# Four transformer layers and a fifth block on one core: the last two output units of the stick-breaking mixers cut in halves around the last group's values

## The reference, cut to what matters

```python
for i in range(4):                                   # then second_block(...)
    mod = silu(c) @ ada_w[i] + ada_b[i]              # 1024 -> 6 * 1024
    sh1, sc1, g1, sh2, sc2, g2 = split(mod, 6)
    h = rms_norm(x, gain[i, 0]) * (1 + sc1) + sh1
    x = x + g1 * mixer(h)                            # i = 0, 3: stick breaking; 1: MoBA; 2: sliding window
    h = rms_norm(x, gain[i, 1]) * (1 + sc2) + sh2
    x = x + g2 * ((silu(h @ w_gate) * (h @ w_up)) @ w_down)

def stick_breaking(h, w_in, w_out):                  # 16 heads of 64
    q, k, v = split(h @ w_in, 3)
    z = q @ k.T / 8
    later = reversed_cumsum(log_keep) - log_keep     # log_keep = log_sigmoid(-z), past keys only
    a = exp(log_sigmoid(z) + later)                  # strictly past keys
    return (a @ v) @ w_out
```

## Time and profile before

| what | value |
|---|---|
| time, median of 3 runs (lowest to highest) | 2160.32 us (2155.64 to 2163.41) |
| the profiled execution: time, span | 2167.3 us, 2165.5 us |
| mean granted TensorE clock | 0.954 |
| TensorE matmul busy | 1952.9 us (90%) |
| VectorE busy | 1344.4 us (62%) |
| ScalarE busy | 918.1 us (42%) |
| GpSimd busy | 111.8 us (5%) |
| matmuls, vector, scalar instructions | 13890, 1412, 1367 |

### The profile page before, as it was taken

One profiled execution on the slowest core, in us unless ns is written; L12 is line 12 of the kernel. 1 busy time (PEld: TensorE's weight loads), 2 busy tenths in 40 slices (PEclk: granted clock), 3 DMA queues, 4 the chain that ended last, 5 costly groups with the idle time before them and its releaser, 6 DMA issues.

```text
span 2165.5 us, 33122 instructions
## 1 busy us (share of the span) xinstructions
PE 1952.9 (90%) x13890; PEld 1522.8 (70%) x13890; DVE 1344.4 (62%) x1412; ACT 918.1 (42%) x1367; POOL 111.8 (5%) x139
## 2 busy tenths in 40 slices
PE   4888999999999998999999899989998888778998
PEld 3665887645687764677777677777786787666877
DVE  6775787453588734688755578875447645445564
ACT  3445444332544324544355544444335211335443
POOL 1001000020100000000000100002000220000000
PEclk9998999999899999999999899998989999989999
DMA  8763898533499931599843267973222000224552
GB/s 325 268 221 95 286 335 323 174 123 116 143 336 315 326 104 59 185 339 314 308 132 121 89 225 254 336 269 128 67 78 78 3 4 4 81 97 149 178 178 97
DMA packets 215114, 393.37 MB, mean 182 GB/s; under 512 B 11306, under 2 KB 130102, under 8 KB 199606
## 3 DMA queue, kind: packets, MB, share of 16 engines
q1 hardware_dynamic: 214453, 391.12, 52.5%
q0 software_dynamic: 512, 0.13, 0.0%
HBM read 390.17 MB, written 1.05 MB: 181 GB/s over the span
## 4 chain that ended last, share of the span: by engine, by line
PE 57%; DVE 25%; ACT 10%; issue 6%; DMA 2%; DVEq 0%; POOL 0%; ACTq 0%; SPq 0%; POOLq 0%
PE G L2126 11%; PE G L2128 11%; DVE w_lo L1426 11%; PE G L2127 11%; DVE acc L1477 6%; PE G L2332 5%; ACT w_hi L931 5%; PE G L2408 2%; PE A L2702 2%; DVE act_st L1760 1%; ACT full L996 1%; DMA raw<-in_ffn_w_down 1%; PE A L2714 1%; PE G L2716 1%; PE A L2174 1%
## 5 line engine op out<-in xcount | busy, mean ns | idle before, releaser
L1426 DVE TENSOR_TENSOR w_lo<-raw,w_hi 128x2048 fp32r<-128x2048 f32 (+2 forms) x237 | 513.4, 2166 | 288.9 <-ACT w_hi L931 277.4
L931 ACT CAST w_hi<-raw 128x2048 fp32r<-128x2048 f32 (+1 forms) x230 | 427.6, 1859 | 553.8 <-PE G L2128 474.7
L2126 PE MATMUL G<-w_hi,h_hi 128*128 128x512 f32 (+2 forms) x1232 | 495.2, 402 | 22.3 <-issue 11.3
L2127 PE MATMUL G<-w_lo,h_hi 128*128 128x512 f32 (+2 forms) x1232 | 485.2, 394 | 0.0
L2128 PE MATMUL G<-w_hi,h_lo 128*128 128x512 f32 (+2 forms) x1232 | 484.8, 394 | 0.0
L1477 DVE SCALAR_TENSOR_TENSOR acc<-raw,c_col,acc 128x2048 f32<-128x2048 f32 x120 | 282.0, 2350 | 20.9 <-DVE w_lo L1426 9.0
L2126 PEld LDWEIGHTS G<-w_hi,h_hi 128*128 128x128 f32 x1232 | 238.5, 194 | 78.4 <-issue 32.7
L2126 PE MATMUL G<-w_hi,act_hi 128*128 128x512 f32 (+2 forms) x640 | 255.4, 399 | 38.1 <-DVE w_lo L1426 28.5
L2128 PEld LDWEIGHTS G<-w_hi,h_lo 128*128 128x128 f32 x1232 | 237.5, 193 | 50.0
L2127 PEld LDWEIGHTS G<-w_lo,h_hi 128*128 128x128 f32 x1232 | 238.2, 193 | 45.9
L2128 PE MATMUL G<-w_hi,act_lo 128*128 128x512 f32 (+2 forms) x640 | 250.2, 391 | 0.0
(11 more groups left out here) (396 smaller groups left out, 2083.9 us busy)
## 6 DMA issues: line engine op xcount, KB each, us to landing
raw<-in_ada_w SPq DMA_DIRECT2D x96, 1024.0 KB, 5.5
raw<-in_ffn_w_gate SPq DMA_DIRECT2D x88, 512.0 KB, 4.0
raw<-in_ffn_w_up SPq DMA_DIRECT2D x88, 512.0 KB, 5.1
raw<-in_ffn_w_down SPq DMA_DIRECT2D x40, 1024.0 KB, 6.5
raw<-in_w_mlp SPq DMA_DIRECT2D x32, 1024.0 KB, 5.4
raw<-in_w_ada SPq DMA_DIRECT2D x24, 1024.0 KB, 5.3
raw<-in_w_in SPq DMA_DIRECT2D x18, 1024.0 KB, 5.3
raw<-in_sb_w_in SPq DMA_DIRECT2D x32, 512.0 KB, 4.6
```

The source lines that it names most:

```text
L931: nc.scalar.copy(w_hi[:, c % 2, 0:len(kts), 0:n], raw[:, slot].rearrange("p (k n) -> p k n", k=UNIT_K)[:, 0:len(kts), 0:n])\
L1426: return nc.vector.tensor_tensor(w_lo[:, c % 2, ks, 0:n], raw[:, slot].rearrange("p (k n) -> p k n", k=UNIT_K)[:, ks, 0:n], w_hi[:, c % 2, ...
L2126: nc.tensor.matmul(banks[t][:, 0:n], x_hi[:, kt, ts], w_hi[:, u % 2, i, 0:n], start=st, stop=False)
L2127: nc.tensor.matmul(banks[t][:, 0:n], x_hi[:, kt, ts], w_lo[:, u % 2, i, 0:n], start=False, stop=False)
```

## The change

- In an sb mixer the first gate's sums (`"r1"`) stand ahead of unit 12 instead of behind unit 13, and ScalarE's copies of them in slot 11 instead of 13. Before T and S of group 3 TensorE waits until they are copied, since these use the same banks.
- Units 14 and 15 are each cut in two halves of 12 matmuls. First the halves with blocks 4 and 5 (group 2) of both units, then V of group 3, then the second gate's sums (`"r2"`), then the halves with blocks 6 and 7 (group 3) of both units. `gemm_done` for each unit comes behind its second half.
- `("V", 3)` moves from slot 13 to slot 14 in `SB_SLOTS`, for TensorE, ScalarE and VectorE alike.
- `ADA_MIX[0]` puts two modulation products in slot 0 and two in slot 5, where it had three in slot 0 and one in slot 5. The products of slots 1 to 4 have indices one lower than before; from slot 6 on they are the same.

```diff
--- before.py
+++ after.py
@@ -417,7 +417,7 @@
 
         SB_SLOTS = {2: [("T", 0)], 3: [("S", 0)], 4: [("C", 0)], 5: [("T", 1)], 6: [("V", 0), ("S", 1)], 7: [("C", 1)],
                     8: [("V", 1), ("T", 2)], 9: [("S", 2)], 10: [("C", 2)], 11: [("V", 2)], 12: [("T", 3), ("S", 3)],
-                    13: [("C", 3), ("V", 3)]}
+                    13: [("C", 3)], 14: [("V", 3)]}
         MOBA_PE = {2: [("N", 0)], 3: [("T", 0)], 4: [("N", 1), ("S", 0)], 5: [("T", 1)], 6: [("N", 2), ("C", 0)], 7: [("S", 1)],
                    8: [("N", 3), ("T", 2), ("C", 1)], 9: [("S", 2)], 10: [("T", 3)], 11: [("V", 0), ("C", 2), ("V", 1)],
                    12: [("V", 2), ("S", 3)], 13: [("C", 3)], 14: [("V", 3)]}
@@ -570,7 +570,7 @@
         ADA_MIX = [{}, {}, {}, {}]
         ADA_FF = [{}, {}, {}, {}]
         for i in range(2 * KT):
-            ADA_MIX[0].setdefault(max(0, i - 2), []).append((0, KT + i))
+            ADA_MIX[0].setdefault((0, 0, 1, 2, 3, 4, 5, 5, 6, 7, 8, 9, 10, 11, 12, 13)[i], []).append((0, KT + i))
         for l in range(DEPTH):
             twice = KT if l + 1 == LAT else 0
             for i in range(ADA_U):
@@ -1146,8 +1146,8 @@
                             squares()
                         for step, g in SB_SLOTS.get(n, []):
                             step_sb(step, g)
-                        if n in (nq + 1, nq + 2):
-                            modulation(l, ("r1", "r2")[n - nq - 1])
+                        if n in (nq - 1, nq + 2):
+                            modulation(l, "r1" if n < nq else "r2")
                     else:
                         for step, g in ACT_STEPS[kind].get(n, []):
                             step_softmax(step, g, kind)
@@ -2356,20 +2356,43 @@
                     unit(h_hi, h_lo, range(4 * h, 4 * h + 4), G[2 * (pns[-1] % 2):2 * (pns[-1] % 2) + 2], h == 0, h == 1,
                          width(panels[pi]), ready=ready_at(f_h, h))
                     steps(n)
+                modulation(l, "r1")
                 po = [k.panel("dve"), k.panel("dve")]
-                n = 2 * len(panels)
-                for h in range(2):
-                    pe.wait_ge(split_lo, f_o[2 * h + 1] - k.native)
-                    for j in range(2):
-                        if h == 0:
-                            wait_panel_free(po[j])
-                        unit(act_hi, act_lo, range(4 * h, 4 * h + 4), G[2 * (po[j] % 2):2 * (po[j] % 2) + 2], h == 0, h == 1, tiles=h == 1 and j == 1)
-                        steps(n)
-                        if n == 2 * len(panels) + 1:
-                            modulation(l, "r1")
-                        if n == 2 * len(panels) + 2:
-                            modulation(l, "r2")
-                        n += 1
+                nq = 2 * len(panels)
+                pe.wait_ge(split_lo, f_o[1] - k.native)
+                for j in range(2):
+                    wait_panel_free(po[j])
+                    unit(act_hi, act_lo, range(4), G[2 * (po[j] % 2):2 * (po[j] % 2) + 2], True, False)
+                    if j == 0:
+                        pe.wait_ge(mod_out, k.sums)
+                    steps(nq + j)
+
+                def half_unit(j, g):
+
+                    u = nth_converted[k.u + j]
+                    pe.wait_ge(hi_ready, u + 1)
+                    pe.wait_ge(lo_ready, u + 1)
+                    for t in range(NT):
+                        bank, ts = G[2 * (po[j] % 2) + t], slice(t * P, t * P + P)
+                        for i in range(2):
+                            kt, part = 2 * g + i, 2 * (g - 2) + i
+                            nc.tensor.matmul(bank, act_hi[:, kt, ts], w_hi[:, u % 2, part], start=False, stop=False)
+                            nc.tensor.matmul(bank, act_hi[:, kt, ts], w_lo[:, u % 2, part], start=False, stop=False)
+                            ins = nc.tensor.matmul(bank, act_lo[:, kt, ts], w_hi[:, u % 2, part], start=False, stop=g == 3 and i == 1)
+                        if g == 3 and j == 1 and t == 0:
+                            ins.then_inc(tile_done, 1)
+                    if g == 3:
+                        ins.then_inc(gemm_done, 1)
+
+                pe.wait_ge(split_lo, f_o[2] - k.native)
+                for j in range(2):
+                    half_unit(j, 2)
+                steps(nq + 2)
+                modulation(l, "r2")
+                pe.wait_ge(split_lo, f_o[3] - k.native)
+                for j in range(2):
+                    half_unit(j, 3)
+                k.u += 2
 
             def softmax_mixer(l, kind):
 
```

## The result

The changed kernel takes 2162.11 us (median of 22 runs, 2156.87 to 2171.55), the kernel before 2159.86 us in the runs beside it (22 runs, 2146.52 to 2165.70). The ratio is 1.0022, 95% interval 1.0012 to 1.0033: slower by about 4.8 us (2.6 to 7.1), within the 0.3% that the prediction called no change, though with 22 runs of each the interval leaves out 0. (The two medians alone differ by 2.3 us, the two means by 4.2; this document goes by the recorded ratio and its interval.) The forecast was +3.6 us, 2163.9.

What follows compares the result with a forecast made beforehand. TensorE was taken to set the pace, so the change is worth what it alters in TensorE's stops. Terms -4.3 + 0 + 4.8 + 3.1 = +3.6 us gave 2163.9 against the median, range 2155 to 2172.

Steps and rivals of the forecast that it cites:

- First slots, -4.3 us: Layer 0, slot 0: two products instead of three start unit 2 2.6 us earlier and avoid a 1.7 us clock loss.
- the first slots give nothing: Rival, chance 0.12: unit 3's load or cast in layer 0 takes back the 4.3 us; total +7.9, 2168.2 us.
- Slot 5, 0: Layer 0: the product moved ahead of kT's copy makes VectorE 0.6 late but costs TensorE 0; without cover, 2.6 us.
- Sums ahead, layer 0: 0, layer 3: +1.7: First gate's sums before unit 12: free in layer 0's 2.23 us idle time, +1.7 us in layer 3, which has no stop.
- Halves, layer 3: +4.8 with the sums: Units 14 and 15 around V of group 3: right half of the norm starts at 1228.5 against 1223.69, +4.8 us.
- wait for `w_lo` 4.2: Layer 3: TensorE idles 4.2 us before unit 15's first half, until its cast and subtraction finish; before, 3.0.
- V's end to the first group 3 half 2.1: Layer 3: the split of V takes 2.1 us before the group 3 halves start, covering the second gate's 1.73.
- that half to the right residual 7.1: Layer 3: rest of unit 14 (2.9), left residual (2.6) and squares (1.6) put the right half 7.1 us later.
- Halves, layer 0: +3.1: Units 14 and 15 around V of group 3: right half of the norm starts at 198.95 against 195.87, +3.1 us.
- `n_st`, 0: Norm behind slot 15: one of two `n_st` is hit by GpSimd's clearing in either kernel; 0, bounds ±1.9 a layer.
- the first `n_st` goes free: Rival, chance 0.13: the first `n_st` escapes GpSimd's clearing, -1.9 us in each layer; total -0.1, 2160.2 us.
- The clock rival, +10.1: Rival, chance 0.17: 1.2 GHz lasts through second half, V and second gate's sums; total +10.1 us, 2170.4.

Runs made afterwards that it cites:

- e1: The kernel before with only the changed ADA_MIX[0] table (two modulation products in slots 0 and 5): 2158.79 us against 2158.59, ratio 0.9998.
- e8: The kernel before with only the changed ADA_MIX[0] table, run again on another chip: 2152.90 us against 2158.52, ratio 0.9976.
- e7: The kernel before with only the first gate's sums moved ahead of unit 12: one execution of 2159.06 us.
- e2: The changed kernel with the old ADA_MIX[0] table, so the second edit alone: 2167.55 us against 2158.59 for before, ratio 1.0039.
- e5: The changed kernel with GpSimd's last two clearings held until the norm's scaled rows are done: 2160.92 us against 2158.52 for before, ratio 1.0010.
- e4: The kernel before with the new ADA_MIX[0] and, on TensorE alone, only unit 14 halved around V of group 3: 2148.17 us against 2158.59, ratio 0.9945.
- e9: Before with new ADA_MIX[0], unit 14 alone halved, GpSimd's clearing late, and VectorE's slot 12 kT copy ahead of the modulation product: one execution, 2142.26 us.

## Why the prediction came out right

**First slots, -4.3 us: right.** TensorE's stop fell to 1.13 us and the stretch behind it ran at 1.00 where 0.76 stood; unit 2 started at 54.69, forecast 54.4. The whole is 4.4 us by the date of V of group 2, and 3.5 by the timings of e1 and e8. The rival "the first slots give nothing" is out.

**Slot 5, 0: right.** The two products stand at 88.53 and 91.10; the copy of kT, reckoned to start 2.6 late, and the split of V follow, and at V of group 2 the first edit's gain is whole on the mean of the kernels.

**Sums ahead, layer 0: 0, layer 3: +1.7: right as the change makes it.** In layer 0 unit 12 starts 3.78 us behind V of group 2, before it was 3.80. The 1.7 of layer 3 is e7's 1.68. My expectation for e7 alone was wrong by 3 us, for the second stop.

**Halves, layer 3: +4.8 with the sums, measured +5.25** (57.62 - 52.37; in e2 +6.0). The steps: wait for `w_lo` 4.2 forecast, 3.81 measured; clock 1.7, measured 1.7; V's end to the first group 3 half 2.1, measured 2.1; that half to the right residual 7.1, measured 1220.64 - 1213.32 = 7.3. No step is off by more than 0.4. (Behind V the working has a slip that changes nothing: from 1209.7 to 1211.73 are 2.0 us, not 2.1.)

**Halves, layer 0: +3.1, whose steps hold and whose base doesn't.** Wait 6.6 forecast, 6.38 measured; clock 2.8, measured 5.35 x 0.50 + 3.86 x 0.09 = 3.0; the residual 195.16 - 187.88 = 7.3 us behind the half. The table has +2.0 (63.4 - 61.4), and after had luck in S of group 3, which took 1.88 us to unit 13 where it took 3.44 before: +3.5 without that. (Of the nine profiles with the same stop ahead of S, after's is the only one in which S kept the full clock.) But before's own profile was a long one behind V: against e1 and e8 it lost 2.8 us to the clock instead of 1.5 and 1.6, and its second `n_st` took 2.62 instead of 1.15 and 0.88. Against these two, with S alike, the halves cost +6.1 and +6.3. I had taken one execution's 2.8 and 2.62 as the kernel's. By e1 and e8 as the base the whole change sums to -4.4 + 5.25 + 6 = +7, by before's own profile to -4.4 + 5.25 + 3.5 = +4.4; timed is +4.8 (2.6 to 7.1). So the mechanism held step by step, but that the total came out within 1.2 us of the timed one is in part luck: layer 0's base scatters by 4 us from execution to execution (61.4, 58.7, 57.1), the forecast had only the highest of them to go by, and the interval is wide enough for either sum.

**`n_st`, 0: right for the profiled execution of before, and its rival "the first `n_st` goes free" is out.** The first one took 2.62 us in layer 0 and 2.76 in layer 3, so it did not go free. Against e1 and e8 it is up to 1.7 us in layer 0, inside the bound of 1.9 given.

**The clock rival, +10.1: not seen in after.** The low level ended in the half (layer 3) or just behind it (layer 0); V and the sums ran at 1.00 and 0.91. It is near, though: in e2 and e5 the whole half of layer 3 ran at 0.50, and V came 0.9 us later there. Two of three kernels with this order lost that, so the forecast's 1.7 for layer 3 is at the lucky end.

## What to carry to other kernels

When a stop of the bound engine is to be filled with other work, date the operands of the filling work too: here they were converted behind the very instruction that ends the stop, and the fill became a longer wait. Fill a stop with what is already converted, or move the conversion into an idle time of its engine ahead of the releaser (ScalarE had 5.8 us). Do not take work from behind a stop to put it ahead: it may be the cover of the next one.

## What the runs showed of the hardware

**A clearing on GpSimd holds VectorE's `n_st` until it ends, even when `n_st` was recorded first.** With s the date of `n_st` less that of the clearing beside it, in us:

| s | `n_st` | clearing | `n_st` ends behind the clearing |
|---|---|---|---|
| -0.81 (before, layer 0) | 0.75 | 1.81 | -1.87 |
| -0.62 (e4, layer 0) | 0.76 | 1.88 | -1.74 |
| -0.47 (e7, layer 3) | 2.84 | 1.82 | +0.55 |
| -0.38 (after, layer 3) | 2.76 | 1.82 | +0.56 |
| -0.24 (before, layers 0 and 3; after, layer 0) | 2.62 | 1.82 | +0.56 |
| -0.11 (e4, layers 0 and 3) | 2.49 | 1.82 | +0.56 |
| +0.19 (before, layer 1) | 2.15 | 1.80 | +0.54 |
| +0.69 (after, layer 2) | 1.66 | 1.80 | +0.55 |
| +1.20 (e1, layer 0) | 1.15 | 1.80 | +0.55 |
| +1.47 (e8, layer 0) | 0.88 | 1.80 | +0.55 |

From -0.47 on the end is the clearing's plus 0.55, whatever the start: `n_st`, which takes 0.75 us by itself, does its work from about 0.2 us ahead of the clearing's recorded end. At -0.62 it went free and the clearing was the one that grew, from 1.81 to 1.88. The page "SBUF — State Buffer" of the Trainium skill, section "SBUF: two separate sides", has the pair of ports as an exclusive lock, which the last column bears out; its rule that whichever starts first gets the pair doesn't fit the recorded starts between -0.47 and -0.11. A subtraction of two tensors did not grow: in layer 3 of before `w_lo` (128x2048) was recorded 0.72 us behind the start of a clearing (1215.09 against 1214.37) and took 2.29 us, as it does elsewhere.

**Behind stops of 2.2 to 2.4 us the clock went either way.** Unit 12 of layer 0, behind 2.21 us of stop, in e1 and then in e8, which are one kernel:

```profile
148.58:154.00 5.42, 5.42 (x24) 4.51 (x25) 5.19 (x3) 1.84 (x2) 0.00 (x0) 1.00 0.75 281
```

```profile
146.34:153.40 7.06, 7.06 (x24) 5.67 (x25) 6.61 (x4) 1.84 (x2) 0.00 (x0) 0.76 0.83 301
```

Over all profiles with that stop, unit 12 lost in one of six (e8). S of group 3 in layer 0, behind 2.39 us in before and 2.42 in after:

```profile
160.46:163.80 3.34, 3.34 (x19) 2.45 (x20) 0.00 (x0) 0.00 (x0) 0.00 (x0) 0.50 1.06 369
```

```profile
157.77:159.60 1.83, 1.83 (x19) 1.48 (x20) 0.00 (x0) 0.00 (x0) 0.00 (x0) 1.00 1.07 392
```

Over all nine profiles with that stop, S took 3.24 to 3.48 us in eight and 1.88 in after. The stop of 1.13 us in after's first slots was not followed by the low level; those of 2.96 and more ahead of V or a half were, in every row shown. The page "TensorE: Matmul & The Clock Gate" of the Trainium skill, section "HAM oscillation — how this bites in real kernels", warns of short bursts between waits, and these rows agree; what the rows add is that one kernel at one stop loses 1.6 us in one execution and nothing in another. In e8 that loss cost nothing in the end, since S was bound by VectorE.

**A wait that the profile puts down to "issue" can be another engine's.** The 2.4 us ahead of S were VectorE's copy of kT, as e9 shows. The 1.13 us in after's slot 0 look to be of the same kind, though no run tests it: the low part of unit 2 ends at 52.30 + 2.29 = 54.59, 0.10 us ahead of the matmul.
